# Down projection of the routed experts in seven block products instead of eight, on one Trainium2 core

## What is computed

```
gates = sum(one_hot(top_i, N_EXPERTS) * softmax(top_v)[..., None], axis=1)
for e in range(N_EXPERTS):          # 8 experts, D_FF_EXPERT = 3584, D_MODEL = 1024
    y = y + gates[:, e:e + 1] * ((silu(x @ we_gate[e]) * (x @ we_up[e])) @ we_down[e])
```

## Time and profile before

| | |
|---|---|
| median of 3 runs | 1348.17 us (1346.59 to 1348.51) |
| the profiled execution, its own time | 1349.45 us |
| its span, first to last instruction | 1347.6 us |
| mean granted TensorE clock | 0.995 |
| TensorE busy | 1318.0 us, 98% of the span |
| VectorE busy | 333.0 us, 25% |
| ScalarE busy | 239.4 us, 18% |
| GpSimd busy | 34.8 us, 3% |
| DMA, mean over the span | 350 GB/s |

### The profile page before, as it was taken

The page is one execution under the profiler, slowest core; times in us unless marked ns, Lnnn a source line. Parts: engine busy times, 40 slices in busy tenths (PEclk is TensorE's granted clock), DMA queues, the critical chain, the costliest instruction groups (busy, mean ns, idle before and its releaser), DMA issues.

```text
span 1347.6 us, 27487 instructions
## 1 busy us (share of the span) xinstructions
PE 1318.0 (98%) x12378; PEld 669.7 (50%) x12378; DVE 333.0 (25%) x546; ACT 239.4 (18%) x381; POOL 34.8 (3%) x66
## 2 busy tenths in 40 slices
PE   6999999999999999999999999999999999999996
PEld 4858799998958533333333333433333333333332
DVE  4336655555445511001001101101100110111313
ACT  3334644443334400000000000000000000000001
POOL 0120000000030000000000000000000000000000
PEclk9999999999999999999999999999999999999998
DMA  9898985564683999999999999999999999999990
GB/s 350 324 353 317 358 302 190 194 203 146 240 290 144 420 378 421 387 394 398 420 414 402 421 414 396 421 351 385 416 421 415 404 421 412 394 421 419 417 382 33
DMA packets 113610, 471.35 MB, mean 350 GB/s; under 512 B 10123, under 2 KB 48821, under 8 KB 77654
## 3 DMA queue, kind: packets, MB, share of 16 engines
q1 hardware_dynamic: 111152, 463.80, 87.4%
q10 hardware_dynamic: 1766, 3.70, 0.7%
q0 software_dynamic: 576, 2.10, 0.4%
HBM read 465.43 MB, written 4.13 MB: 348 GB/s over the span
## 4 chain that ended last, share of the span: by engine, by line
PE 95%; DVE 3%; ACT 1%; issue 1%; DMA 0%; POOL 0%; SPq 0%; DVEq 0%; ACTq 0%; POOLq 0%
PE ps L2180 43%; PE ps L2195 21%; PE ps L1770 4%; PE ps L1771 4%; PE ps L1772 4%; PE ps L1720 2%; PE ps L1818 2%; PE ps L1991 1%; PE ps L1992 1%; PE ps L1993 1%; PE ps L1783 1%; PE ps L1784 1%; PE ps L1785 1%; PE ps L2106 1%; PE ps L1743 1%; PE ps L1919 1%
## 5 line engine op out<-in xcount | busy, mean ns | idle before, releaser
L2180 PE MATMUL ps<-ering,xg 128*32 128x512 f32 (+1 forms) x6144 | 579.0, 539 | 0.0
L2180 PEld LDWEIGHTS ps<-ering,xg 128*32 128x32 f32 x6144 | 199.5, 110 | 378.4 <-issue 378.3
L2195 PE MATMUL ps<-ering,eT 128*32 128x512 f32 x2688 | 290.7, 592 | 0.0
L2195 PEld LDWEIGHTS ps<-ering,eT 128*32 128x32 f32 x2688 | 87.0, 110 | 197.8 <-issue 197.8
L1577 DVE TENSOR_TENSOR sq<-sg,ps 128x512 f32<-128x512 f32 (+1 forms) x48 | 29.8, 621 | 463.9 <-PE ps L2180 461.8
L1092 DVE TENSOR_TENSOR low<-ring,high 128x1024 fp32r<-128x1024 f32 (+1 forms) x104 | 122.6, 1202 | 71.3 <-ACT high L778 71.3
L1030 ACT ACTIVATE sg<-ps 128x512 f32<-128x512 f32 (+1 forms) x48 | 26.2, 545 | 541.5 <-PE ps L2180 541.5
L1770 PE MATMUL ps<-hx,high 128*128 128x256 f32 x432 | 120.0, 278 | 2.4 <-DVE hx L1146 2.4
L1772 PE MATMUL ps<-hx,low 128*128 128x256 f32 x432 | 119.7, 277 | 0.0
L1771 PE MATMUL ps<-hx,high 128*128 128x256 f32 x432 | 119.7, 277 | 0.0
L778 ACT ACTIVATE high<-ring 128x1024 fp32r<-128x1024 f32 (+1 forms) x104 | 104.9, 1038 | 53.6 <-PE ps L1772 29.5
(11 more groups left out here) (258 smaller groups left out, 919.0 us busy)
## 6 DMA issues: line engine op xcount, KB each, us to landing
ering<-in_moe_w_down SPq DMA_DIRECT2D x112, 1024.0 KB, 12.0
ering<-in_moe_w_gate SPq DMA_DIRECT2D x64, 1024.0 KB, 9.4
ering<-in_moe_w_up SPq DMA_DIRECT2D x64, 1024.0 KB, 11.5
ering<-in_moe_w_gate SPq DMA_DIRECT2D x64, 768.0 KB, 7.8
ering<-in_moe_w_up SPq DMA_DIRECT2D x64, 768.0 KB, 9.3
ring<-in_w_ada SPq DMA_DIRECT2D x40, 1024.0 KB, 7.6
ring<-in_ffn_w_gate SPq DMA_DIRECT2D x11, 1024.0 KB, 6.6
ring<-in_ffn_w_up SPq DMA_DIRECT2D x11, 1024.0 KB, 8.9
```

The source lines that it names most:

```text
L2180: last = mm(ps[32 * c:32 * c + 32, bank, 0:width].rearrange("p (n r) -> p n r", r=64), xg[:, kk, at, 32 * g:32 * g + 32], w[t][:, c, :, :] ...
L2195: last = mm(ps[32 * group:32 * group + 32, bank, :], eT[s][:, g, 2 * i + odd, :], w[:, odd, 512 * half:512 * (half + 1)], start=(s, i) == ...
```

## The change

For slot groups 0 and 1, both halves of a block's rows and both halves of the outputs, the product of a 2 x 2 matrix of blocks (A, hidden) with a 2 x 2 matrix of blocks (B, weights) is computed in Strassen's form (Winograd's variant): seven block products m1 to m7 of sums of A and sums of B. Slot group 2 keeps its four products (h0a, h0b, h0c in the first output half, h1a, h1b in the second). That is `down_seven`, 11 matmuls per block where `down` has 12. It is used in experts 0 to 6; expert 7 keeps `down`.

What this adds:
- VectorE forms three weight sums per block (`sum_weights`, all 128 x 512): S1 = b12 - b11, S2 = b22 - S1, S3 = b21 - S2, each from the one before, into four places (wsum); place x is free again when the matmul that reads it has finished (wsum_used). The sums of block 0 and the first of block 1 stand ahead of the multiplications of step 1, the others behind them.
- GpSimd forms the fourth, b22 - b12 (128 x 512), into two places (wdif); that of block n waits until block n - 2 is done.
- VectorE forms four sums of the hidden values per step (`sum_hidden`).
- m5, m6 and m4 wait for a sum (wsum_ready), m7 for GpSimd's (wdif_ready). The first down matmuls wait for the first up bank of step 1 (bank 5 is now written by the down projection), so the last kk of step 1 takes the slot groups in the order 2, 0, 1.
- Y_row is put together from three banks (5, 6, 7), with more and smaller operations on both engines, and slot group 2 of the next expert's first gate matmuls waits until ScalarE has copied bank 5.
- The copies behind a gather are all ScalarE's (four per turn), VectorE's `take_group` is gone.
- Some semaphores are merged (cleared for ones_set, pads_set, silu_zero; x_router_in; small_in), with the same waits. The row of zeros in y_rows is stored early.

The diff, cut to this:

```diff
+G_ORDER = ((0, 1, 2), (2, 0, 1))
...
+DOWN_PLACE = {"m1": (5, 2), "m2": (6, 0), "m3": (7, 0), "m4": (6, 1), "m5": (7, 1), "m6": (7, 3), "m7": (5, 3),
+              "h0a": (5, 0), "h0b": (6, 3), "h0c": (6, 2), "h1a": (5, 1), "h1b": (7, 2)}
+DOWN_TURNS = (("m2", "m5", "m1", "m6", "m3", "m4", "h0c", "m7", "h0a", "h1a", "h1b"),
+              ("h0b", "m2", "m5", "m1", "m6", "m3", "m4", "h1b", "m7", "h0a", "h1a"),
+              ("m1", "h0b", "m2", "m5", "h1b", "m6", "m3", "m4", "h1b", "m7", "h0a"),
+              ("m5", "m1", "m6", "m2", "m4", "h0c", "m7", "m3", "h1a", "h1b", "h0b"))
+W_SUMS = 3
+W_PLACES = 4
...
+        wsum = nc.alloc_sbuf_tensor_at("wsum", [128, W_PLACES, 512], f32, offset=token_rows_at)
+        wdif = spare[:, 0:2, :]
+        Y_a, Y_b = spare[:, 0, :], spare[:, 1, :]
...
+        n0, n1 = (w // 64 for w in E_WIDTH)
+        h_s2 = (cst[:, C_ROT:C_ROT + 32 * n0].rearrange("p (i t) -> p i t", t=32), h_last[:, 0, :].rearrange("p (i t) -> p i t", t=32))
+        h_s3 = (cst[:, C_ROT + 32 * n0:C_ROT + 64 * n0].rearrange("p (i t) -> p i t", t=32), h_last[:, 1, :].rearrange("p (i t) -> p i t", t=32))
+        h_s4 = (hm[:, :, 384:384 + 16 * n0].rearrange("p a (j t) -> p a j t", t=32), sg[:, :, 384:384 + 32 * n1 // SG].rearrange("p a (j t) -> p a j t", t=32))
...
+        def quarters(n):
+            w = ering[:, E_PLACE[E_ITEM["d", 0, 0] + n]:E_PLACE[E_ITEM["d", 0, 0] + n] + SLOT].rearrange("p (r n) -> p r n", r=2)
+            return w[:, 0, 0:512], w[:, 0, 512:1024], w[:, 1, 0:512], w[:, 1, 512:1024]
...
+            for k in range(NE - 1):
+                pool.wait_ge(Y_row_ready, 1 + 2 * k)
+                for n in range(BLOCKS):
+                    t = BLOCKS * k + n
+                    arrived_quarters(pool, k, n)
+                    if n >= 2:
+                        pool.wait_ge(pieces_used, k * E_ITEMS + (MP0 + E_ITEM["d", 0, 0] + n - 1))
+                    b11, b12, b21, b22 = quarters(n)
+                    nc.gpsimd.tensor_tensor(wdif[:, t % 2, :], b22, b12, ALU.subtract).then_inc(wdif_ready, 1)
...
-                    for m in (0, 1):
+                    for m in range(4):
...
-                if k > 1:
-                    act.wait_ge(Y_row_stored, 16 * k)
-                A(Yt[0:64, :], ps[0:64, 7, :], ACT.Copy).then_inc(Y_row_even, 1)
-                A(Y_row[64:CAP, 512:1024], ps[96:128, 6, :], ACT.Copy).then_inc(Y_row_ready, 1)
-                act.wait_ge(Y_row_ready, 3 * k)
-                if k == 1:
-                    act.dma_start(y_rows[ROWS_KEPT:ROWS_KEPT + 1, :], token_rows[0:1, 0, :]).then_inc(Y_row_stored, 16)
+                A(Yt[:, :], ps[:, ROWS_BANK_FIRST, :], ACT.Copy).then_inc(Y_row_even, 1)
+                act.wait_ge(Y_row_even, 2 * k - 1)
+                A(Y_a[0:32, :], Yt[64:96, :], ACT.Copy)
+                A(Y_b[64:96, :], Yt[32:64, :], ACT.Copy).then_inc(Y_row_even, 1)
+                act.wait_ge(Y_row_ready, 1 + 2 * k)
                 act.dma_start(y_rows[CAP * (k - 1):CAP * k, :], Y_row[0:CAP, :]).then_inc(Y_row_stored, 16)
...
-                if k > 1:
-                    dve.wait_ge(Y_row_stored, 16 * k)
-                V.tensor_copy(Y_row[0:CAP, 0:512], ps[0:CAP, 6, :]).then_inc(Y_row_ready, 1)
-                dve.wait_ge(Y_row_even, k)
-                V.tensor_tensor(Y_row[0:64, 512:1024], ps[64:128, 7, :], Yt[0:64, :], ALU.add).then_inc(Y_row_ready, 1)
+                dve.wait_ge(Y_row_even, 2 * k - 1)
+                u2 = Y_b[96:128, :]
+                step(V.tensor_tensor(u2, ps[96:128, 7, :], Yt[64:96, :], ALU.add))
+                V.tensor_tensor(Y_a[64:96, :], ps[96:128, 6, :], Yt[0:32, :], ALU.add)
+                V.tensor_tensor(Y_a[32:64, :], u2, Yt[96:128, :], ALU.add)
+                V.tensor_tensor(Y_b[32:64, :], u2, Yt[96:128, :], ALU.add)
+                step(V.tensor_tensor(Y_b[0:32, :], ps[32:64, 7, :], u2, ALU.add))
+                dve.wait_ge(Y_row_even, 2 * k)
+                dve.wait_ge(Y_row_stored, 16 * k)
+                V.tensor_tensor(Y_row[0:CAP, 0:512], ps[0:CAP, 6, :], Y_a[0:CAP, :], ALU.add).then_inc(Y_row_ready, 1)
+                V.tensor_tensor(Y_row[0:CAP, 512:1024], ps[0:CAP, 7, :], Y_b[0:CAP, :], ALU.add).then_inc(Y_row_ready, 1)
...
+            def sum_weights(k, n, j):
+                at = W_SUMS * (BLOCKS * k + n) + j
+                b11, b12, b21, b22 = quarters(n)
+                before = wsum[:, (at - 1) % W_PLACES, :]
+                if j == 0:
+                    arrived_quarters(dve, k, n)
+                else:
+                    dve.wait_ge(wsum_ready, at)
+                if at >= W_PLACES:
+                    dve.wait_ge(wsum_used, at - W_PLACES + 1)
+                x, y = ((b12, b11), (b22, before), (b21, before))[j]
+                V.tensor_tensor(wsum[:, at % W_PLACES, :], x, y, ALU.subtract).then_inc(wsum_ready, 1)
...
+            def sum_hidden(s, j):
+                a11, a12, a21, a22 = (hidden(s, g, odd) for g in range(2) for odd in range(2))
+                if j == 0:
+                    V.tensor_tensor(h_s3[s], a11, a21, ALU.subtract)
+                elif j == 1:
+                    step(V.tensor_tensor(a21, a21, a22, ALU.add))
+                elif j == 2:
+                    step(V.tensor_tensor(h_s2[s], a21, a11, ALU.subtract))
+                else:
+                    split = dict(a=(2, SG)[s])
+                    parts = (x.rearrange("p (a j) t -> p a j t", **split) for x in (a12, h_s2[s]))
+                    V.tensor_tensor(h_s4[s], *parts, ALU.subtract).then_inc(h_sums_ready, 1)
...
+                        if not rnd and not ends:
+                            if s == 0:
+                                dve.wait_ge(eT_ready, k * NSTEP * SG + SG)
+                                for j in range(4):
+                                    sum_hidden(0, j)
+                                for j in range(W_SUMS):
+                                    sum_weights(k, 0, j)
+                                sum_weights(k, 1, 0)
+                            else:
+                                for n in range(1, BLOCKS):
+                                    for j in range(n == 1, W_SUMS):
+                                        sum_weights(k, n, j)
+                                    if n == 3:
+                                        dve.wait_ge(eT_ready, k * NSTEP * SG + NSTEP * SG)
+                                    if 3 <= n < 7:
+                                        sum_hidden(1, n - 3)
+                    if rnd and not ends:
+                        take_xg(gathers_before(e + 1, rnd))
...
+                            if kk == 0 and g == SG - 1 and not begins and not rnd and s == 0:
+                                pe.wait_ge(Y_row_even, 2 * k - 1)
...
+                    def down_seven(s, i):
+                        n = (0, n0)[s] + i
+                        t = BLOCKS * k + n
+                        b11, b12, b21, b22 = quarters(n)
+                        arrived_quarters(pe, k, n)
+                        if i == 0:
+                            pe.wait_ge(eT_ready, k * NSTEP * SG + (s * SG + SG))
+                            pe.wait_ge(h_sums_ready, 2 * k + s + 1)
+                        if n == 0:
+                            pe.wait_ge(eh_ready, k * NSTEP * SG + SG + 1)
+                        s4 = h_s4[s][:, i // (4, 2)[s], i % (4, 2)[s], :]
+                        sums = [wsum[:, (W_SUMS * t + j) % W_PLACES, :] for j in range(W_SUMS)]
+                        factors = {"m1": (hidden(s, 0, 0)[:, i, :], b11), "m2": (hidden(s, 0, 1)[:, i, :], b21), "m3": (s4, b22),
+                                   "m4": (hidden(s, 1, 1)[:, i, :], sums[2]), "m5": (hidden(s, 1, 0)[:, i, :], sums[0]),
+                                   "m6": (h_s2[s][:, i, :], sums[1]), "m7": (h_s3[s][:, i, :], wdif[:, t % 2, :])}
+                        left = {"h0": [(hidden(s, 2, odd)[:, i, :], b) for odd, b in enumerate((b11, b21))],
+                                "h1": [(hidden(s, 2, odd)[:, i, :], b) for odd, b in enumerate((b12, b22))]}
+                        for x, name in enumerate(DOWN_TURNS[n % 4]):
+                            if name in ("m5", "m6", "m4"):
+                                pe.wait_ge(wsum_ready, W_SUMS * t + ("m5", "m6", "m4").index(name) + 1)
+                            elif name == "m7":
+                                pe.wait_ge(wdif_ready, t + 1)
+                            h, w = factors[name] if name in factors else left[name[0:2]].pop(0)
+                            bank, group = DOWN_PLACE[name]
+                            last = mm(ps[32 * group:32 * group + 32, bank, :], h, w, start=(n, x) in DOWN_BEGINS, stop=(n, x) in DOWN_ENDS, skip_group_check=True)
+                            if name in ("m5", "m6", "m4"):
+                                last.then_inc(wsum_used, 1)
                         last.then_inc(pieces_used, 1)
...
+                            if rnd or ends:
+                                down(s, i)
```

(40 more changed lines are left out.)

65 lines of the change are left out of this document (36 added, 29 removed).

## The result

The changed kernel takes 1388.28 us (median of 4 runs, 1386.34 to 1389.92) against 1348.34 us before (1346.59 to 1348.89): a ratio of 1.0299, 95% interval 1.0286 to 1.0312. It is slower by 40 us, inside the forecast range and 5 us under the forecast of 1393.

A forecast was written before the change was run, and what follows sets the result against it. TensorE bounded the kernel before; with the change VectorE's chain, lengthened by GpSimd, sets down at 44.0 us: +39.8 in five experts, +3.0 and +1.6 in experts 0 and 3, +44.4 in all, forecast 1393 us, range 1363 to 1424.

The forecast's parts named there:

- What bounds the kernel, and what TensorE saves: Whole kernel: TensorE bounds it; 98 fewer matmuls in down save 21.0 us, 3.0 per expert, leaving 33.05 us of down.
- goes round the four column groups as the old one did: Down matmuls: the new table of places keeps the old order of column groups, so a matmul's pace stays at 0.215 us.
- What they cost each other: Down: VectorE's two-input sums and GpSimd's subtraction exclude each other, each GpSimd operation adding 1.1 us to VectorE's chain.
- The terms of the sum for one expert: Down part: transpose 1.3, sums 27.0, hidden sums 1.4, GpSimd 13.2 and last matmuls 1.1 make 44.0 us.
- the four places for sums do not bind: VectorE's sums in down: a place is asked for about 4 x 1.0 us later and is free by then.
- The two experts with gathers: Experts 0 and 3: down with gathers grows by 3.0 us in expert 0 and 1.6 in expert 3.
- VectorE goes on meanwhile: Down of expert 0: VectorE keeps working during gathers, so TensorE's own 37.8 us fit under 44.0.
- What costs nothing: Sums ahead of step 1, Y_row's assembly and store, ScalarE's copies and merged semaphores: all hidden under other work, no added time.
- The side-by-side rival: Down: VectorE and GpSimd do not exclude each other, so the kernel gains up to 21.0 us, 1327 to 1331; 14%.
- The clock: TensorE in down: the clock falls as it waits; at half clock 30 us more per down part, 1560 us; 2%.

The follow-up runs named there:

- e4_no_sums: Changed kernel without any weight sums of VectorE or GpSimd, m4 to m7 reading quarters of the weights as they are (incomplete result): 1334.76 us, ratio 0.9903.
- e1_no_fourth: Changed kernel without GpSimd's fourth weight sum, m7 reading quarter b22 itself without a wait (incomplete result): 1334.76 us, ratio 0.9897.
- e3_pool_writes: Changed kernel with GpSimd's subtraction replaced by two memsets of the same place, same waits and semaphore (incomplete result): 1334.32 us, ratio 0.9891.
- e5_psum_input: Changed kernel with ScalarE copying one input of VectorE's down weight sums to PSUM; experts 0 and 3 keep twelve matmuls: 1337.17 us, ratio 0.9922.
- e7_fourth_twice: Changed kernel with GpSimd's subtraction done twice per block, one behind the other, same result: 1469.61 us, ratio 1.0903.

## Why the prediction was right, point by point

**What bounds the kernel, and what TensorE saves.** Right. The 33.05 us for 154 matmuls are in the chain of e4_no_sums to the digit. Not foreseen was the half round: "goes round the four column groups as the old one did" holds within a down part, but 154 is not a multiple of four. It costs 0.43 us per expert, and it is in the changed kernel too: there TensorE waits for no sum from 680.71 on, its 57 records end at 680.71 + 6.62 = 687.33, and the next gate starts 0.44 us later, at 687.77.

**What they cost each other.** Right, and it decides the sign. The step from a few small operations of the mixers to the experts held: whoever comes second waits to the end of the other's instruction. The experiments isolate it from both sides: remove GpSimd's reading (e1_no_fourth, e3_pool_writes) or one of VectorE's SBUF reads (e5_psum_input), and the sums are at 0.69 us. The rule of the Trainium skill ("SBUF — State Buffer", Who interferes with whom) names the same conditions: two SBUF inputs on VectorE, a GpSimd instruction that reads. Here both conditions were seen to be necessary.

**The terms of the sum for one expert.** 44.0 us forecast, 42.9 measured. The start fits (1.3 us forecast; the first sum behind step 1 starts at 646.37, 1.5 after gate and up end). Two terms were too high. A sum was taken as 0.71 us, though of three only two wait for the one before: in e1_no_fourth three of them start 2.06 us apart (657.44 and 659.50 in VectorE's timeline), 38 in 26.1 and not 27.0. GpSimd's operation was taken as 1.1 us; by e7_fourth_twice it is 0.97, so 12 cost 11.6 and not 13.2. With both the sum would be 1.5 + 26.1 + 1.4 + 11.6 + 1.1 = 41.7, 1.2 under the measured. Two things were left out. VectorE waits three times for a free place of the four (0.34, 0.27 and 0.27 us in its timeline), so "the four places for sums do not bind" was not quite true. And the tail is 2.0 us and not 1.1: the last sum ends at 685.74 and the next gate starts at 687.77, as TensorE, which waits for no sum from 680.71 on, is then behind by its own work and by the half round. Together these are 1.8 us for the 1.2 that is missing, so the parts close to 0.6 us and no better. That the total came within 5 us is in part luck: in each expert two terms 2.5 us too high stand against 1.2 us left out, and expert 3 and the last expert, below, cost together 2.5 us more than forecast.

**The two experts with gathers.** "VectorE goes on meanwhile" failed in part: with four places VectorE stops once it is four sums ahead, and the gathers are in the chain. Expert 0 goes from 529.00 to 572.99, 44.0 us, as forecast. Expert 3, with its longer gathers, takes 45.5 from 874.37 to 919.90, where 44.0 were forecast. From gate to gate it is 117.4 us (from 802.53) against 114.5 (786.13 to 900.64 in the chain of the kernel before): 2.9 more than before where 1.6 were forecast.

```profile
874.37 3.83 PE ps L2338 x34
...
912.85 6.62 PE ps L2338 x57
919.54 0.36 PE ps L2338
919.90 71.55 PE ps L2292 x762
```

**What costs nothing.** One cover was overlooked: the assembly of Y_row at the end of expert 6 is followed by its store, the fetches and the added rows, and only then by the last expert's first product. In the chain of the changed kernel:

```profile
1269.85 7.42 DMA y_rows<-Y_row
1277.54 9.29 DMA token_rows<-y_rows,rti
...
1305.72 0.70 DVE sq L1673
...
1337.72 36.08 PE ps L2307 x336
```

Expert 7's gate and up take 1337.72 - 1264.34 = 73.4 us for 72.16. Together, by the trace: 5 x 6.6 + 3.0 + 2.9 + 1.2 = 40.1 us, and the span grew by 1388.1 - 1347.6 = 40.5.

**The rivals.** The side-by-side rival, 1327 to 1331, did not come; e1_no_fourth, which makes its condition true, gave 1334.8, so even it was priced 4 to 8 us too well, by the half round, the gathers and the last expert. DMA was 377 GB/s in the down part of expert 1 and bounded nothing. The clock stayed at 1.00 in down, although TensorE was busy for 38.48 of 42.94 us only (windows view of the changed kernel):

```profile
644.83:687.77 42.94, 38.48 (x319) 13.94 (x314) 39.05 (x45) 0.24 (x1) 17.81 (x12) 1.00 0.95 377
```

## What to carry to other kernels

Before work is shared between VectorE and GpSimd, look at their operands and not only at their idle time: here two engines that were nearly idle and had 2.06 and 1.29 us of work for a block of 2.36 could not do it together, as both read SBUF for two-input operations. Add the two up. Giving the work to VectorE alone was better (1356 us for 1388) but still no gain over the 1348 of the kernel before; only with one of VectorE's inputs in PSUM, brought there by an idle ScalarE, did the change pay (1337). A few short overlaps somewhere else in the trace, whose ends lay a fixed time apart, were enough to see this ahead. And where four column groups of TensorE are in turn, count the matmuls between two seams modulo four.
